# One semaphore per half: an expert's gate and up weights as two 2 MB transfers in a mixture-of-experts stage

## The reference

```
def run_block(args):                      # 64 experts, top 2 of each token
    tok, e = args
    xb = t_pad[tok]                       # the tokens routed to expert e
    hb = jax.nn.silu(xb @ w_gate[e]) * (xb @ w_up[e])     # 1024 -> 512, twice
    return hb @ w_down[e]                                 # 512 -> 1024
...
y = jax.ops.segment_sum(yb.reshape(cap, d) * buf_w[:, None], buf_tok, num_segments=n + 1)
```

## Time and profile before

| | |
|---|---|
| median of 3 runs | 1820.82 us |
| lowest, highest | 1818.39, 1821.52 us |
| span of the profiled execution, first to last instruction | 1818.5 us |
| TensorE clock granted, mean over the span | 0.886 of full |
| busy share of the span: PE, DVE, ACT, POOL | 76%, 33%, 26%, 26% |
| moved by DMA | 517.27 MB, 284 GB/s over the span |

### The profile page before, as it was taken

How to read it: one execution, slowest core, us unless ns; L and a number is a source line. 1 busy time by engine, 2 the same in 40 slices (tenths; PEclk the granted TensorE clock), 3 DMA queues, 4 the chain that set the end, 5 groups by cost and what they waited for, 6 DMA issues and landing times.

```text
span 1818.5 us, 31166 instructions
## 1 busy us (share of the span) xinstructions
PE 1376.0 (76%) x13669; PEld 1083.1 (60%) x13670; DVE 597.4 (33%) x892; ACT 480.7 (26%) x783; POOL 466.7 (26%) x105
## 2 busy tenths in 40 slices
PE   6996899989789997997776656575656656575655
PEld 5986789878689997997643333342333333342333
DVE  4376433655846777445311001010101001010102
ACT  4753356435444443441200000000000000000001
POOL 5653114565358775663000000000000000000000
PEclk8988899989989999998789888898889888898878
DMA  7432113433245554346599999999999999999995
GB/s 271 164 111 75 47 47 117 157 130 134 90 155 184 186 185 139 123 156 254 237 429 431 430 429 431 435 428 432 432 428 431 430 429 430 435 429 431 432 428 234
DMA packets 34773, 517.27 MB, mean 284 GB/s; under 512 B 3858, under 2 KB 3986, under 8 KB 4882
## 3 DMA queue, kind: packets, MB, share of 16 engines
q1 hardware_dynamic: 34706, 516.32, 69.7%
HBM read 515.25 MB, written 1.05 MB: 284 GB/s over the span
## 4 chain that ended last, share of the span: by engine, by line
DMA 38%; PE 37%; DVE 17%; ACT 4%; issue 2%; POOL 1%; SPq 0%; DVEq 0%; ACTq 0%
DMA e_gu<-experts 38%; PE psum L770 10%; PE psum L281 6%; PE psum L282 6%; PE psum L283 6%; DVE f_act L1657 3%; DVE all_sq L1322 3%; ACT w_high L871 1%; DVE f_y L1647 1%; PE psum L340 1%; PE psum L471 1%; DVE m_mem L1335 1%; DVE r_qraw L1730 1%; PE psum L487 1%; DVE act_low L1345 1%
## 5 line engine op out<-in xcount | busy, mean ns | idle before, releaser
L1881 POOL TENSOR_TENSOR w_low<-w_raw,w_high 128x2048 fp32r<-128x2048 f32 x101 | 466.5, 4623 | 384.0 <-ACT w_high L871 383.9
L770 PE MATMUL psum<-e_gu,x_xt 128*32 128x256 f32 x4096 | 297.3, 455 | 247.0 <-DMA e_gu<-experts 231.3
L770 PEld LDWEIGHTS psum<-e_gu,x_xt 128*32 128x32 f32 x4096 | 147.0, 130 | 389.2 <-DMA e_gu<-experts 253.8
L281 PE MATMUL psum<-h_high,w_high 128*128 128x256 f32 x1024 | 297.5, 291 | 23.0 <-DVE h_low L1332 22.5
L282 PE MATMUL psum<-h_low,w_high 128*128 128x256 f32 x1024 | 292.8, 286 | 0.0
L283 PE MATMUL psum<-h_high,w_low 128*128 128x256 f32 x1024 | 292.6, 286 | 0.0
L871 ACT ACTIVATE w_high<-w_raw 128x2048 fp32r<-128x2048 f32 x101 | 193.1, 1914 | 84.6 <-PE psum L283 74.1
L281 PEld LDWEIGHTS psum<-h_high,w_high 128*128 128x128 f32 x1024 | 198.3, 194 | 25.9 <-issue 24.4
L282 PEld LDWEIGHTS psum<-h_low,w_high 128*128 128x128 f32 x1024 | 198.5, 194 | 0.5 <-issue 0.2
L283 PEld LDWEIGHTS psum<-h_high,w_low 128*128 128x128 f32 x1024 | 198.3, 194 | 0.0
L1858 DVE COPY x_yb<-psum 128x256 f32<-128x256 f32 x64 | 27.2, 425 | 425.9 <-PE psum L806 425.9
(11 more groups left out here) (403 smaller groups left out, 1998.9 us busy)
## 6 DMA issues: line engine op xcount, KB each, us to landing
e_gu<-experts SPq DMA_DIRECT2D x64, 4096.0 KB, 23.9
e_dn<-experts SPq DMA_DIRECT2D x64, 2048.0 KB, 25.1
w_raw<-dense SPq DMA_DIRECT2D x101, 1024.0 KB, 4.8
all_c<-c SPq DMA_DIRECT2D x1, 2099.5 KB, 15.8
r_c<-c SPq DMA_DIRECT2D x1, 1344.0 KB, 5.9
all_x<-x_t SPq DMA_DIRECT2D x1, 1024.0 KB, 4.9
m_mem<-mem_t SPq DMA_DIRECT2D x1, 1024.0 KB, 5.0
out_t<-all_h SPq DMA_DIRECT2D x4, 256.0 KB, 2.6
```

The source lines that it names most:

```text
L281: mm(ps, w[0], src[0], start=start, stop=False, **kw)
L770: last = mm(half(psum[32 * s:32 * s + 32, GU_BANK[j % 2], 0:256], P), X["xt"][:, k, CAP * j:CAP * (j + 1)], expert_gu[PLACE[j]][:, k, :, s ...
L1881: nc.gpsimd.tensor_tensor(low(name), raw[:, place(name), :], high(name).bitcast(F32), ALU.subtract).then_inc(sem("w_low"), 1)
```

## The change

An expert's gate and up weights are loaded by two transfers of 2 MB instead of one of 4 MB. The first brings input chunks 0 to 3 and the second chunks 4 to 7; each has a semaphore of its own for each buffer. `gate_up` waits for the first before chunk 0 and for the second before chunk 4. A partition's share of each transfer is now 16 KB in one piece. SyncE's wait before the load is as it was, and so are the down loads, the buffers and the order of everything.

```diff
             def gate_up(i, j):
 
-                pe.wait_ge(sem(f"gu_loaded{PLACE[j]}"), loads(j, i))
                 for k in range(DC):
+                    if k % 4 == 0:
+                        pe.wait_ge(sem(f"gu_{('lo', 'hi')[k // 4]}_loaded{PLACE[j]}"), loads(j, i))
                     for s in range(4):
                         last = mm(half(psum[32 * s:32 * s + 32, GU_BANK[j % 2], 0:256], P),
...
             def load_gate_up(e, j):
 
-                sp.dma_start(expert_gu[PLACE[j]].rearrange("p c g f -> p (c g f)"),
-                             experts_in[bass.ds(e, 1), :, 0:2 * SLOT].rearrange("a p w -> p (a w)")
-                             ).then_inc(sem(f"gu_loaded{PLACE[j]}"), 16)
+                for hf, part in enumerate(("lo", "hi")):
+                    sp.dma_start(expert_gu[PLACE[j]][:, 4 * hf:4 * hf + 4].rearrange("p c g f -> p (c g f)"),
+                                 experts_in[bass.ds(e, 1), :, hf * SLOT:(hf + 1) * SLOT].rearrange("a p w -> p (a w)")
+                                 ).then_inc(sem(f"gu_{part}_loaded{PLACE[j]}"), 16)
```

## The result

The changed kernel takes 1821.95 us (median of 20 runs, 1819.99 to 1825.4) and the kernel before, in 20 runs beside it, 1818.95 us: a ratio of 1.0017 with a 95% interval of 1.0010 to 1.0024. A second comparison, on another occasion and with 10 and 32 runs, gave 1.0026 (1.0016 to 1.0035). The forecast was 1822.5 us, or 1.7 us more than a median of 1820.82 from three runs of the kernel before. With more runs that median is lower, 1818.95, and the difference is the better measure: by the medians it is 3.0 us in the first comparison and 5.1 in the second (4.7 by its ratio). So it lies about where the bound of 0.2% was drawn, on the slow side.

A forecast was written before the change was run, and what follows sets the result against it. The prediction took the DMA queue's rate to bound the kernel from about 902 us. Loop 3.7, waits 0.2 and end -2.2 gave +1.7 us on 1820.82, so 1822.5 us (own range 1821.3 to 1824.4; 8 in 10: 1818.8 to 1827).

The forecast's parts named there:

- The sum: Whole kernel: loop cost 3.7, extra waits 0.2 and end gain -2.2 make +1.7 us.
- The bound: Expert loop from about 902 us: the DMA queue's rate sets the time; starting `gate_up` early is worth nothing there.
- More transfers: Expert loop: the split costs 0.06 us for each of 61 experts in the full queue, 3.7 us.
- The extra waits on TensorE: Two `gate_up` ahead of 902 us, weights already landed: two more waits cost 0.2 us, bounds 0 and 0.6.
- The end: Last expert: the down product starts earlier, waiting only for the down weights; gain 2.2 us.
- the two sums of 4.7 and 4.88 us: Last expert, after gate and up land: product ready 3.25 to 4.7 us later, down weights 4.88 us later.
- Rival A: End: TensorE at half clock slows down product, scatter and norm's sums, up to 6.8 us more; chance 0.16.
- one of the signs of being wrong: End: TensorE's clock at half after the last landing would show the prediction wrong.
- B: Loop: `gate_up` is on the path, -87 us, or milder, transfers pass at lowest spacing, -7 us; together chance 0.04.
- C: Loop: the queue does not hide a fixed cost of 4.8 us per second half, 293 us more; chance 0.02.
- D: Loop and end: the split costs nothing and only the end gains, -2.0 us, 1818.8; chance 0.14.
- E: Loop: the upper price, from 0.1 us per expert, +4.1 us or more, 1824.9; chance 0.09.

The follow-up runs named there:

- e10: The changed kernel run once more, unaltered, against the kernel before: 1824.86 us, ratio 1.0026.
- e11: The kernel before run again as if it were another kernel, against itself: 1819.08 us, ratio 0.9995.
- e4: The kernel before with every `gate_up` computed twice into the same bank: 1830.53 us, ratio 1.0059 to the kernel before.
- e1: The changed kernel, but the product waits for both 2 MB transfers before its first chunk: 1824.93 us, ratio 1.0029 to the kernel before.
- e2: The kernel before, still one 4 MB transfer and one semaphore, but made of two 16 KB pieces per partition: 1824.46 us, ratio 1.0031.
- e7: The changed kernel with eight matmuls of zeros ahead of the last norm's sums: 1820.66 us, ratio 1.0008 to the kernel before.
- e12: The changed kernel with eight matmuls of zeros ahead of the last norm's sums, the same kernel as e7: 1822.3 us, ratio 1.0014 to the kernel before.
- e3: The changed kernel with four 1 MB transfers for gate and up, waits still per half: 1834.82 us, ratio 1.0082 to the kernel before.
- e6: The kernel before with the split for the last expert of the last turn alone: 1820.96 us, ratio 1.0008 to the kernel before.
- e9: The kernel before with the last expert alone split and eight matmuls of zeros at the end: 1818.47 us, ratio 0.9993.

## Why the prediction held, point by point

*The sum.* Of 3.7 + 0.2 - 2.2 = +1.7 us the ledger shows 4.2 + 0 - 2.1, and 1.4 more of the tail, for which the sum had nothing: +3.5 (e10 against e11: 4.8 - 2.1 + 1.4 = +4.1). The forecast time, 1822.5 us, lies 0.6 us from the 1821.95 measured, although the sum was 1.8 us short by the ledger, and that is luck: the three runs of the kernel before that it was added to had a median 1.9 us above that of twenty. As a difference, the first comparison (+3.0) lies inside the forecast's +0.5 to +3.6, and the second (+5.1, or 4.7 by its ratio) outside.

*The bound.* Right. e4 shows that TensorE is off the path in the loop, and e1 that the early half is worth nothing there.

*More transfers, 61 x 0.06 = 3.7 us.* The mechanism was right and the size low. The spacing of landings had said 0.045 per expert and the packet times 0.13; the sum had 0.06. The pitches show 0.080, and the stream grew by 4.2 to 5.1 us (four profiles of the changed kernel, filled or not, 899.98 to 900.51; three of the kernel before 895.41 to 895.80). The landings are given to 0.1 us, and the 0.045 was twice the down spacing less that of the 4 MB, which doubles the error of the former. e2 names the unit that I had left open: it is the packet, not the transfer.

*The extra waits on TensorE, 0.2 us.* They cost nothing: 901.39 - 894.22 = 7.17 us from the first `gate_up` to the first issue, for 902.47 - 895.29 = 7.18 before.

*The end, -2.2 us.* Right in size: -2.1. The second piece ran mostly at half clock (3.51 us, at 0.53), and the product was ready about when the down weights landed, as the two sums of 4.7 and 4.88 us had it. Which of the two comes last is a tie: the profile puts the last gap to ScalarE's copy here and in e10 (0.39 and 0.37 us), and to the down transfer, as forecast, in e7 and e12 (0.68 and 0.58), where the second piece took 3.23 and 3.32 us.

*Rival A, the clock at the end.* It came true for a part. The sentence of the prediction that held it to a chance of 0.16 expected the down product and the scatter to be hit as well; both ran at full clock (1.94 and 1.15 us), and only the norm's sums, behind a thin stretch, fell: +1.4 us, under the 1.9 from which it would have decided alone. It is most of the 1.8 us between the forecast of +1.7 and the ledger's +3.5; the price per packet is the other part. With it came one of the signs of being wrong, a half clock after the last landing: the two products right behind the landing didn't have it, the start of the sums did. In e3 the down product was hit as well, and the tail grew by 4.4 us. The reason that I gave, the broken product, is not what decides: e1, e2 and e4 have an unbroken one, and their tails grew by 1.7 us. What does is open. The Trainium skill (TensorE: Matmul & The Clock Gate, section HAM oscillation) warns that pieces shorter than the wait before them run throttled. The rows here mostly agree: the piece after 3.48 us of waiting took 3.52 us and the last one, after 2.96, took 3.51, while the pieces after 1.38 and 1.18 us, waits shorter than the piece, took 1.93 at full clock. But the down product of the last expert but one also took 1.93 us, behind a wait of 2.01.

*Rivals B and C* are refuted by e4 and by the pitch: a second transfer of 2 MB adds 0.080 us to an expert, and not microseconds. The fixed cost of about 2.0 us that the prediction took from the Trainium skill (DMA: Bandwidth & Descriptors, section Anatomy of one DMA) is fitted there to transfers that GpSimd issues, and those here are SyncE's. *D* is refuted by e1: the split does cost something. *E* is nearly what happened to the loop (0.08 per expert for 0.10); its sum of +4.1 is above the first comparison (+3.0) and under the second (+5.1).

## What to carry to other kernels

When a stage runs at the rate of the DMA queue, as this loop does, a transfer split for an earlier start buys one thing, the lag behind the last landing, and is paid for at every transfer: count the packets that it adds to each engine, and split only where the product really waits behind the queue, at the end. Even that was here a gain of the ledger alone, 2.1 us: e6 and e9 are not shown to be faster than before. Before you believe an engine's share in a chain of waits, compare the time to landing in the loop with that on an empty queue; the difference is the slack that a faster engine would only lengthen. And where the change is worth 2 us, look at the clock of the few unhidden products at the end, since it moved as much as the change did.

## What the runs showed of the hardware

The price of a packet is steady: 8 more data packets per engine and expert cost 0.078 us (e2), 24 more with three more transfers 0.235 us (e3), about 10 ns a packet whether the piece is cut to 16 KB or to 8 KB. Before the runs I had not expected a short stretch of idle TensorE to matter as it does at the end: with 1.33 us busy in the 3.6 us before, the norm's sums ran at 0.72 of full clock and took 5.10 us, and eight matmuls of zeros in that stretch brought them back to 3.72 at 1.00. The same thin stretch stands in the kernel before, whose sums took 3.72 us in two profiles out of two without the zeros. Its windows (columns as in the earlier trace rows), the stretch and the sums:

```profile
1802.60:1806.20 3.60, 1.33 (x21) 0.90 (x21) 3.48 (x10) 0.69 (x2) 0.00 (x0) 1.00 0.00 0
1806.20:1809.90 3.70, 3.70 (x16) 2.96 (x16) 1.07 (x2) 3.22 (x5) 0.00 (x0) 1.00 0.00 0
```
